# The first modulation in four quarters, and u, k and q in another order, in a hybrid S5, attention and expert block

## The chip, the cores and the metric

One core of one Trainium2 chip runs the whole kernel. It has five engines that run side by side and wait for each other by semaphores: TensorE (PE), VectorE (DVE), ScalarE (ACT), GpSimd (POOL) and SyncE (SP), which here issues nearly all loads. The metric is the device time of one execution in microseconds (us). The time before is 1171.37 us, the median of 3 runs.

## The reference

One block on x (256 tokens x 1024) with a conditioning vector c. The part that matters here is its opening:

```python
cond = jax.nn.silu(c)
mod = cond @ w_ada[l] + b_ada[l]
sh1, sc1, gt1, sh2, sc2, gt2 = jnp.split(mod, 6, axis=-1)
h = modulate(rms_norm(x, g_mix[l]), sh1, sc1)     # h * (1 + sc1) + sh1
proj = h @ w_in[l]                                # [u | q | k | v | gate_A | gate_B], 4096 columns
# u -> S5: complex diagonal state space model, scan over positions
# q, k, v -> 8 heads of causal attention with partial rotary
# then gates, one output projection, and a top-4-of-32 expert FFN
```

All arithmetic is f32. Each weight is read once, some 460 MB in all.

## The kernel before, in words

The program is written engine by engine; the order of the code is the order of execution on each engine, and semaphores link them. Weights come through `ring`, 12 slots of 1 MB: `order` is the order in which SP loads pieces, `use_order` that in which PE uses them up, and SP loads into a slot when its last piece is used.

The first modulation (shift and scale, 2048 columns of w_ada) comes in 8 pieces `("first", 0..7)`, in two halves of four: `first_products(a)` multiplies a piece by `condb` (silu(c), 32 equal columns) in 16 matmuls of 32 x 128 (two records each in the profile). When a half is complete, ACT copies its row out of PSUM (`first_row_copy`), PE turns it into columns (`first_columns`, L550), DVE adds the bias and makes the scale (`first_modulation`, L1448 and L1452), and DVE and ACT make two slices each of `hT`, the modulated x with the model dimension on partitions (L1457 on DVE, `first_hidden` L1155 on ACT). They read x that PE has transposed (`x_columns`, L557).

`proj(g, h)` multiplies one half of the 8 slices k of hT by the weights of group g: 0 is u, 1 q, 2 k, 3 v, 4 to 7 the gates (L609, for v L606). Each slice k of a group is 4 matmuls of 128 x 256 (two records each in the profile). ACT copies a finished group to SBUF (`projected`, L1167). q and k are rotated: PE makes the turned part (`rotate`, L669), DVE combines it with cos and sin (`rotary`, L1494 to L1501).

For the S5 branch, DVE and POOL make tables of cos and sin, `ecos` and `esin`, DVE for the states' first half (LOW) and POOL for the second (HIGH). Level n squares (`square`, L271 to L275) and doubles (`double`, L285 to L290) the table, n = 2, 4, ... 128; at n = 128 the doubling is two rounds of six operations. POOL waits for `phases`, which DVE sets when its own table is finished, before POOL doubles at 128, because of a shared scratch. DVE also makes the discretised B (L1479 to L1481: six operations of 128 x 256, from loaded constants `const_in` and `sprm`); ACT lays it out in blocks (`Bblk`, L1197), PE transposes these (`b_columns`, L650), ACT copies them out. `b_u(j)` (L626) feeds the scan of DVE (`recurrence`).

The small parameters of the S5 branch are turned by PE (L574) and copied by DVE into `sprm` (L1442), which both tables start from.

Behind all this come the gates and the attention, the output projection, and then a loop over the experts, whose weights stream through the same memory.

## Time and profile before

| | |
|---|---|
| median of 3 runs | 1171.37 us (1171.29 to 1172.31) |
| span of the profiled execution | 1171.2 us |
| PE busy | 1126.0 us, 96% |
| DVE busy | 452.4 us, 39% |
| ACT busy | 138.2 us, 12% |
| POOL busy | 107.8 us, 9% |
| moved by DMA | 460.06 MB, mean 393 GB/s |

The profile is that of one execution. The engines overlap, so their busy times do not add up to the span. A timeline row gives the start, the time from the first to the last end of a merged group, the engine, the line and the operation, and in brackets how long the engine was idle before it and what ended this. SPq and ACTq are the issues of DMAs from these engines. Matmuls overlap in the record, so their rate is read from starts, or from a long group: 96 in 20.96 us are 0.218 us each.

### The profile page before, as it was taken

How to read it: one execution, taken by the hardware profiler on the slowest of the kernel's cores; microseconds unless marked ns; L12 is line 12 of the kernel's file. 1: busy time of each engine (PE TensorE's matmuls, PEld its weight loads, DVE VectorE, ACT ScalarE, POOL GpSimd, SP SyncE). 2: the span in 40 equal slices, each digit the busy share in tenths (PEclk: the TensorE clock that was granted, in tenths of full speed). 3: DMA queues.
4: the chain of work that ended last, by engine and by line, in shares of the span. 5: the costliest groups of instructions: out<-in, count | busy, mean ns of one | idle time of the engine just before them, and what ended most of it. 6: DMA issues, size and time to landing. Idle time of an engine off the chain costs nothing.

```text
span 1171.2 us, 17315 instructions
## 1 busy us (share of the span) xinstructions
PE 1126.0 (96%) x7011; PEld 501.6 (43%) x7011; DVE 452.4 (39%) x960; ACT 138.2 (12%) x299; POOL 107.8 (9%) x142
## 2 busy tenths in 40 slices
PE   6999999999999999999999999999999999999996
PEld 5877788554333333333333333333333333333331
DVE  5897767462232222333322232222222222222323
ACT  3213231141000000001000000000000000000002
POOL 2868730000000000000000000000000000000000
PEclk9999999999999999999999999999999999999998
DMA  9993379979999999999999999999999999999994
GB/s 345 317 381 116 108 270 380 418 296 420 428 428 429 430 429 430 431 431 431 435 430 430 430 430 430 431 430 431 431 431 430 430 430 432 433 430 426 426 427 191
DMA packets 49230, 460.06 MB, mean 393 GB/s; under 512 B 8958, under 2 KB 9410, under 8 KB 26924
## 3 DMA queue, kind: packets, MB, share of 16 engines
q1 hardware_dynamic: 48176, 458.19, 93.7%
q10 hardware_dynamic: 1020, 1.38, 0.4%
q8 instruction: 25, 0.41, 0.1%
q14 instruction: 9, 0.07, 0.0%
HBM read 458.51 MB, written 1.05 MB: 392 GB/s over the span
## 4 chain that ended last, share of the span: by engine, by line
PE 74%; DMA 21%; DVE 2%; ACT 1%; issue 1%; SPq 1%; DVEq 0%
PE ps L1038 27%; DMA ring<-in_w_gu 16%; PE ps L1080 16%; PE ps L609 8%; DMA ring<-in_w_down 4%; PE ps L1013 4%; PE ps L957 3%; PE ps L806 2%; PE ps L1060 2%; PE ps L824 2%; PE ps L789 1%; PE ps L881 1%; PE ps L606 1%; DMA ring<-in_w_ada 1%; PE ps L1068 1%
## 5 line engine op out<-in xcount | busy, mean ns | idle before, releaser
L1080 PE MATMUL ps<-ring,tmp 128*64 128x512 f32 x1024 | 227.2, 595 | 11.9 <-ACT tmp L1293 9.7
L1038 PE MATMUL ps<-ring,zone 128*64 128x512 f32 x1024 | 227.2, 596 | 11.1 <-DMA ring<-in_w_gu 11.1
L1038 PE MATMUL ps<-zone 128*64 128x512 f32 x1024 | 227.2, 596 | 0.2 <-DVE zone L1725 0.2
L1792 DVE TENSOR_TENSOR x_tok<-x_tok,ps 128x512 f32<-128x512 f32 x128 | 82.0, 682 | 262.4 <-PE ps L1013 258.9
L1080 PEld LDWEIGHTS ps<-ring,tmp 128*64 128x64 f32 x1024 | 82.8, 137 | 135.6 <-issue 130.8
L1038 PEld LDWEIGHTS ps<-ring,zone 128*64 128x64 f32 x1024 | 70.6, 137 | 163.4 <-issue 142.7
L1038 PEld LDWEIGHTS ps<-zone 128*64 128x64 f32 x1024 | 70.5, 137 | 153.1 <-issue 146.2
L1290 ACT ACTIVATE hT<-hT 128x256 f32<-128x256 f32 x64 | 23.9, 417 | 726.5 <-DVE hT L1807 726.5
L609 PE MATMUL ps<-hT,ring 128*128 128x256 f32 x448 | 101.5, 382 | 0.9 <-DVE hT L1457 0.9
L1807 DVE TENSOR_SCALAR hT<-ps 128x256 f32<-128x256 f32 x64 | 24.2, 420 | 191.7 <-PE ps L1038 191.7
L609 PEld LDWEIGHTS ps<-hT,ring 128*128 128x128 f32 x448 | 83.5, 190 | 14.4 <-issue 4.0
L1786 DVE TENSOR_TENSOR tmp<-ps,zone 128x512 f32<-128x512 f32 x32 | 22.1, 692 | 164.4 <-PE ps L1080 164.4
L1013 PE MATMUL ps<-tmp,xn_tok 64*128 64x512 f32 x248 | 70.0, 641 | 0.0
L957 PEld LDWEIGHTS ps<-ptmp,zone 128*128 128x128 bf16 x1488 | 45.1, 98 | 23.6 <-issue 23.6
L957 PE MATMUL ps<-ptmp,zone 128*128 128x64 bf16 x1488 | 48.8, 194 | 0.0
L1013 PEld LDWEIGHTS ps<-tmp,xn_tok 64*128 64x128 f32 x248 | 18.7, 185 | 50.3 <-issue 50.3
L824 PE MATMUL ps<-cst,ptmp 32*64 32x512 f32 x256 | 34.8, 613 | 0.0
L1000 PE MATMUL ps<-cst,ptmp 32*64 32x512 f32 x128 | 34.4, 613 | 0.0
L1060 PE MATMUL ps<-cst,ptmp 32*64 32x512 f32 x128 | 34.4, 613 | 0.0
L1293 ACT COPY tmp<-ps 128x256 f32<-128x256 f32 x64 | 20.9, 375 | 85.9 <-PE ps L1068 85.9
L806 PE MATMUL ps<-zone,ring 128*128 128x256 f32 x128 | 28.2, 380 | 0.0
L1814 DVE SCALAR_TENSOR_TENSOR hT<-hT 128x256 f32<-128x256 f32 x64 | 27.2, 425 | 2.3
(328 smaller groups left out, 828.7 us busy)
## 6 DMA issues: line engine op xcount, KB each, us to landing
ring<-in_w_down SPq DMA_DIRECT2D x61, 2048.0 KB, 18.7
zone<-in_w_gu SPq DMA_DIRECT2D x23, 4096.0 KB, 28.5
ring<-in_w_gu SPq DMA_DIRECT2D x23, 4096.0 KB, 32.3
zone<-in_w_gu SPq DMA_DIRECT2D x14, 2048.0 KB, 14.0
ring<-in_w_gu SPq DMA_DIRECT2D x13, 2048.0 KB, 15.0
ring<-in_w_ada SPq DMA_DIRECT2D x24, 1024.0 KB, 13.2
ring<-in_w_in SPq DMA_DIRECT2D x16, 1024.0 KB, 14.2
ring<-in_w_gu SPq DMA_DIRECT2D x10, 1024.0 KB, 9.6
```

Of the source, the lines that this page charges most:

```text
L609: last = mm(ps[:, b + m // 2, (m % 2) * T:(m % 2) * T + T], w[:, kk, P * m:P * m + P], hT[:, k, :], start=(k == 0 and m % 2 == 0), stop=(k ...
L806: last = mm(ps[:, b + m // 2, (m % 2) * T:(m % 2) * T + T], w[:, kk, P * m:P * m + P], gluT[:, kk, :], start=(kk == 0 and m % 2 == 0), sto ...
L824: mm(ps[CAP * h:CAP * h + CAP, b, :], hotb[own, :], brow[own, 512 * h:512 * h + 512], start=True, stop=False, skip_group_check=True)
L957: last = mm(ps[:, 2, CAP * f:CAP * f + CAP], xpart[:, c, i, stored(f)], pick[:, i, :], start=(i == 0 and c == 0), stop=(i == TT - 1 and c ...
L1000: last = mm(ps[CAP * h:CAP * h + CAP, 5, :], hotb[3 * EXPERTS:P, :], brow[3 * EXPERTS:P, 0:2 * T], start=True, stop=True, skip_group_check ...
L1013: mm(ps[:, 6 + h, :], pickwT[half, P * t:P * t + P], ysb[half, :], start=True, stop=True).then_inc(S["comb_up"], 1)
L1038: last = mm(ps[CAP * h:CAP * h + CAP, b, :], hg[:, 2 * j + kk, :], w[:, kk, D * b + 512 * h:D * b + 512 * h + 512], start=False, stop=(j = ...
L1060: last = mm(ps[CAP * h:CAP * h + CAP, 3, :], hotb[own, :], brow[own, 512 * h:512 * h + 512], start=True, stop=False, skip_group_check=True)
L1080: last = mm(ps[CAP * h:CAP * h + CAP, 3, :], actT[:, q, j, :], w[:, q, 512 * h:512 * h + 512], start=False, stop=(j == DN_PIECES - 1 and q ...
L1792: V.tensor_tensor(x_tok[:, t, 512 * h:512 * h + 512], x_tok[:, t, 512 * h:512 * h + 512], ps[:, bank + h, :], ALU.add).then_inc(S["comb_ad ...
L1807: V.tensor_scalar(rows_of(gate[:, pair[g]]), down_pair(ps[:, 0, :], g), LIMIT, None, ALU.min).then_inc(S["gated"], 1)
L1814: V.scalar_tensor_tensor(act_[:, pair[g]], up[:, pair[g]], 1.0, gate[:, pair[g]], ALU.add, ALU.mult).then_inc(S["act_set"], 1)
```

## The change

The first modulation is made in four quarters, each of two pieces. A piece now holds four k slices of 256 shift and 256 scale columns, loaded by two DMAs of 0.5 MB with rows of 1 KB instead of one with rows of 2 KB. The x columns are transposed a quarter (two slices) at a time. The weights of u and q come in joint pieces `("uq", 0..3)`, two slices k of both, with rows of 4 KB; `pair_proj` uses them a slice at a time. The first half of k (`proj(2, 0)`) stands ahead of the modulation's last quarter. Then u is finished, then k, then q: ACT copies k before q, and k is rotated first. The banks of PSUM are laid out anew. DVE's square and doubling at 64 and 128 are parted by the modulations of quarters 2 and 3, and the discretised B is made behind the doubling at 128 instead of ahead of it. The bias loads move from ACT's queue to SP's, ahead of the weights; the large constants load two pieces later and in another order. The silu uses exp and a reciprocal on DVE instead of the sigmoid. A row of the S5 parameters is made on POOL. `scores(0)` no longer waits for v, `weigh(0)` does.

```diff
-    order = several("first", 0, 1, 2, 3) + several("in", 0, 2) + several("first", 4, 5, 6, 7) + several("in", 1, *range(3, 15))
+    order = several("first", 0, 1) + several("uq", 0) + several("first", 2, 3) + several("uq", 1) + several("in", 4)
+    order += several("first", 4, 5, 6, 7) + several("uq", 2, 3) + several("in", *range(5, 15))
...
-    use_order = several("first", 0, 1, 2, 3) + several("in", 0) + several("first", 4, 5, 6, 7) + several("in", 2, 1, *range(3, 16))
+    use_order = several("first", 0, 1, 2, 3) + several("uq", 0) + several("first", 4, 5) + several("uq", 1) + several("first", 6, 7)
+    use_order += several("in", 4, 5) + several("uq", 2, 3) + several("in", *range(6, 16))
...
-            half, sc, k4 = n // 4, n % 4 // 2, n % 2
-            return ada[:, 4 * k4:4 * k4 + 4, D * sc + W * half:D * sc + W * half + W]
+            quarter, k4 = n // 2, n % 2
+            both = ada[:, 4 * k4:4 * k4 + 4, 0:2 * D].rearrange("p k (s c) -> p k s c", s=2)
+            return both[:, :, :, T * quarter:T * quarter + T]
+        if kind == "uq":
+            return win[:, 2 * n:2 * n + 2, 0:2 * W]
...
+            sp.dma_start(rows[R_ADA:R_ADA + 2 * KD, :], ada_bias[0:2 * D].rearrange("(k p) -> k p", p=P)).then_inc(more_rows_in, 16)
+            sp.dma_start(rows[R_GMIX:R_GMIX + KD, :], g_mix.rearrange("a (k p) -> (a k) p", p=P)).then_inc(more_rows_in, 16)
+            sp.dma_start(wide_rows[0:8, :], ada_bias[2 * D:6 * D].rearrange("(k p) -> k p", p=RUN * P)).then_inc(more_rows_in, 16)
+            sp.dma_start(wide_rows[8:10, :], g_ffn.rearrange("a (k p) -> (a k) p", p=RUN * P)).then_inc(more_rows_in, 16)
+            sp.dma_start(rows[R_D:R_D + KW, :], ssm_d.rearrange("a (k p) -> (a k) p", p=P)).then_inc(more_rows_in, 16)
...
-                sp.dma_start(slot(n, src.shape[1]), src).then_inc(arrived[n % SLOTS], 16)
+                if kind == "first":
+                    own = slot(n, 4).rearrange("p k (s c) -> p k s c", s=2)
+                    for sc in range(2):
+                        sp.dma_start(own[:, :, sc], src[:, :, sc]).then_inc(arrived[n % SLOTS], 16)
+                else:
+                    sp.dma_start(slot(n, src.shape[1]), src).then_inc(arrived[n % SLOTS], 16)
...
+            for n in range(place["in", 5] + 1):
                 load_piece(n)
-            sp.dma_start(cst[:, P:], const[:, P:]).then_inc(S["const_in"], 16)
             for r, (b, cc) in enumerate(((b_re, c_re), (b_im, c_im))):
                 sp.dma_start(b_in[:, r], b[0].rearrange("(s q) p c -> (q p) s c", q=2)).then_inc(S["const_in"], 16)
                 sp.dma_start(c_in[:, r], cc[0].rearrange("(m g) c p -> (g c) m p", m=KW)).then_inc(S["const_in"], 16)
-            for n in range(place["in", 3] + 1, place["glu", 0]):
+            sp.dma_start(cst[:, P:], const[:, P:]).then_inc(S["const_in"], 16)
+            for n in range(place["in", 5] + 1, place["glu", 0]):
                 load_piece(n)
...
+            def first_columns(quarter):
+
+                pe.wait_ge(S["modrow_sb"], quarter + 1)
+                nc.tensor.transpose(ps[:, 6, mod_cols(quarter)], first_row[quarter], ident).then_inc(S["modT_up"], 1)
+
+            def x_columns(quarter):
+
+                pe.wait_ge(S["xn1"], TT if quarter == 0 else 2 * TT)
+                if quarter == 1:
+                    pe.wait_ge(S["hD_sb"], 1)
+                elif quarter > 1:
+                    pe.wait_ge(S["hD_sb"], quarter)
+                    pe.wait_ge(S["hA_sb"], quarter)
+                    pe.wait_ge(S["mod1_sb"], quarter)
...
+            def pair_proj(g, k, ms=(0, 1, 2, 3)):
+
+                n = take("uq", k // 2)
+                w = slot(n, 2)
+                hidden(k)
+                b = PROJ_BANK[g]
+                if g == 1 and k == 0:
+                    pe.wait_ge(S["sprm_sb"], 1)
+                for m in ms:
+                    last = mm(ps[:, b + m // 2, (m % 2) * T:(m % 2) * T + T], w[:, k % 2, W * g + P * m:W * g + P * m + P], hT[:, k, :],
+                              start=(k == 0 and m % 2 == 0), stop=(k == KD - 1), skip_group_check=True)
+                if g == 0 and k == KD - 1:
+                    last.then_inc(S["u_up"], 1)
+                if g == 1 and k % 2 == 1:
+                    last.then_inc(w_used, 1)
...
-            last.then_inc(more_cols_up, 1)
-            for a in range(1, 3):
-                first_products(a)
-            pe.wait_ge(S["xn1"], TT)
+            last.then_inc(S["cols_up"], 1)
+            first_products(1)
             x_columns(0)
-            first_products(3)
-            pe.wait_ge(S["ssm_rows"], 1)
+            first_columns(0)
+            pe.wait_ge(S["ssm_rows"], 2)
...
-            first_columns(0)
-            x_columns(1)
...
-            proj(0, 0)
+            pair_proj(0, 0)
+            x_columns(1)
+            pair_proj(0, 1)
+            first_products(2)
+            pair_proj(1, 0, (0, 1))
+            first_products(3)
+            pair_proj(1, 0, (2, 3))
+            first_columns(1)
+            pair_proj(1, 1)
+            x_columns(2)
+            pair_proj(0, 2), pair_proj(0, 3)
             first_products(4)
-            for kk in range(3):
-                proj(1, 0, (kk,))
-                first_products(5 + kk)
-            proj(1, 0, (3,), (0, 1))
-            first_columns(1)
-            proj(1, 0, (3,), (2, 3))
-            proj(0, 1)
-            proj(1, 1)
-            proj(2, 0)
+            pair_proj(1, 2)
+            first_products(5)
+            pair_proj(1, 3)
+            first_columns(2)
+            proj(2, 0, (0,))
+            x_columns(3)
+            first_products(6)
+            proj(2, 0, (1,))
+            first_products(7)
+            proj(2, 0, (2,))
+            first_columns(3)
+            proj(2, 0, (3,))
+            for k in range(4, KD):
+                pair_proj(0, k)
+            proj(2, 1)
+            pair_proj(1, 4)
             b_columns()
-            rotate(qT, 0)
+            rotate(kT, 0)
             c_columns(0)
             c_columns(1)
-            proj(2, 1, (0,))
+            pair_proj(1, 5)
             b_u(0)
-            proj(2, 1, (1, 2, 3))
+            pair_proj(1, 6), pair_proj(1, 7)
             proj(3, 0, (0,))
-            rotate(kT, 1)
...
+            act.wait_ge(S["lnD"], 1)
+            link(nc.scalar.activation(stat[:, 1, :], stat[:, 3, :], ACT.Exp))
 
             act.wait_ge(S["cols_sb"], 1)
-            nc.scalar.activation(cond[:, :], cols[:, R_C:R_C + KD], ACT.Sigmoid).then_inc(S["cond_half"], 1)
+            nc.scalar.activation(cond[:, :], cols[:, R_C:R_C + KD], ACT.Exp, scale=-1.0).then_inc(S["cond_half"], 1)
...
                                          scale=cst[:, C_MB + q:C_MB + q + 1]).then_inc(S["Bblk_set"], 1)
-            projected(1, qT)
+            projected(2, kT)
...
                                      scale=(1.0 if r == 0 else -1.0)).then_inc(S[f"CT{r}_sb"], 1)
-            projected(2, kT)
+            projected(1, qT)
             projected(3, v_tok)
...
+            pool.wait_ge(ssm_products, 1)
+            link(nc.gpsimd.tensor_tensor(sprow[:, 13, :], sprow[:, 9, :], are[:, :], ALU.mult))
+            link(nc.gpsimd.tensor_tensor(sprow[:, 14, :], sprow[:, 8, :], aim[:, :], ALU.mult))
+            link(nc.gpsimd.tensor_tensor(sprow[:, 13, :], sprow[:, 13, :], sprow[:, 14, :], ALU.subtract))
+            nc.gpsimd.tensor_tensor(sprow[:, 4, :], sprow[:, 13, :], sprow[:, 10, :], ALU.mult).then_inc(S["ssm_rows"], 1)
...
+                dve.wait_ge(S["mod1_sb"], quarter + 1)
+                k = 2 * quarter
+                V.scalar_tensor_tensor(scale1[:, k:k + 2], mod[:, SC1 + k:SC1 + k + 2], 1.0,
+                                       cols[:, R_GMIX + k:R_GMIX + k + 2], ALU.add, ALU.mult).then_inc(S["scale1_set"], 1)
+                dve.wait_ge(S["scale1_set"], quarter + 1)
+                dve.wait_ge(S["xT_up"], quarter + 1)
+                V.tensor_scalar(hT[:, k, :], xT_bank(k), scale1[:, k:k + 1],
+                                mod[:, SH1 + k:SH1 + k + 1], ALU.mult, ALU.add).then_inc(S["hD_sb"], 1)
...
             dve.wait_ge(S["cols_sb"], 2)
             first_modulation(0)
+            dve.wait_ge(S["sprm_up"], 1)
+            V.tensor_copy(sprm[:, :, :].rearrange("p j s -> p (j s)"), ps[:, 3, 0:5 * ST]).then_inc(S["sprm_sb"], 1)
+            dve.wait_ge(S["sprm_sb"], 1)
             first_phase(V, link, LOW)
             level(2)
-            for n in (4, 8, 16, 32):
+            level(4)
+            first_modulation(1)
+            for n in (8, 16, 32):
                 level(n)
-            first_modulation(1)
-            level(T // 4)
+            square(V, link, T // 4, LOW)
+            first_modulation(2)
+            double(V, link, T // 4, LOW, (tmp[:, 0], tmp[:, 1]))
+            square(V, link, T // 2, LOW)
+            first_modulation(3)
+            double(V, link, T // 2, LOW, (ptmp, probs))
+            V.engine_nop().then_inc(S["phases"], 1)
 
...
-            level(T // 2)
-            V.engine_nop().then_inc(S["phases"], 1)
```

PE from the first weight products on; first the program before. L542 are `first_products`, L557 `x_columns`, L574 the S5 rows, L550 `first_columns`, L609 a projection.

```order
L542 MATMUL ps<-ring,condb 32x128 x16
L562 MATMUL ps<-cst,zone 128x36
L564 MATMUL ps<-cst,zone 128x10 x4
L542 MATMUL ps<-ring,condb 32x128 x32
L557 MATMUL ps<-cst,xn_tok 128x128 x8
L542 MATMUL ps<-ring,condb 32x128 x16
L574 MATMUL ps<-cst,zone 128x16 x5
L550 MATMUL ps<-cst,zone 128x128 x2
L557 MATMUL ps<-cst,xn_tok 128x128 x8
L609 MATMUL ps<-hT,ring 128x256 x16
```

The same place of the changed program, from the second piece on: L567 are `first_products`, L587 `x_columns`, L574 `first_columns`, L622 the S5 rows, L603 `pair_proj`.

```order
L567 MATMUL ps<-ring,condb 32x128 x16
L587 MATMUL ps<-cst,xn_tok 128x128 x4
L574 MATMUL ps<-cst,zone 128x128
L622 MATMUL ps<-cst,zone 128x16 x5
L603 MATMUL ps<-hT,ring 128x256 x4
L587 MATMUL ps<-cst,xn_tok 128x128 x4
L603 MATMUL ps<-hT,ring 128x256 x4
L567 MATMUL ps<-ring,condb 32x128 x16
L603 MATMUL ps<-hT,ring 128x256 x2
L567 MATMUL ps<-ring,condb 32x128 x16
L603 MATMUL ps<-hT,ring 128x256 x2
L574 MATMUL ps<-cst,zone 128x128
```

The first projection stands behind two pieces instead of four, and six pieces and three quarters of the x columns now stand between projections.

DVE from the last half round of the doubling at 128 on, before. L287 to L290 are the doubling, L1484 sets `phases`, L1494 to L1501 are the first rotary (of q).

```order
L287 TENSOR_TENSOR zone<-ptmp,probs 128x4x127
L288 TENSOR_TENSOR ptmp<-zone 128x508
L289 TENSOR_TENSOR probs<-zone 128x508
L290 TENSOR_TENSOR zone<-ptmp,probs 128x4x127
L1484 ISA
L1494 TENSOR_TENSOR tmp<-ps,cst 128x512
L1500 TENSOR_TENSOR zone<-zone,cst 128x512
L1501 TENSOR_TENSOR zone<-zone,tmp 128x512
```

And in the changed program. L294 ends the doubling, L1539 sets `phases`, L1546 to L1548 are the discretised B, L1559 and L1565 the first rotary (of k).

```order
L294 TENSOR_TENSOR zone<-ptmp,probs 128x4x127
L1539 ISA
L1546 TENSOR_TENSOR tmp<-zone,sprm 128x256
L1547 TENSOR_TENSOR tmp<-zone,sprm 128x256
L1548 TENSOR_TENSOR tmp<-tmp 128x256
L1546 TENSOR_TENSOR tmp<-zone,sprm 128x256
L1547 TENSOR_TENSOR tmp<-zone,sprm 128x256
L1548 TENSOR_TENSOR tmp<-tmp 128x256
L1559 TENSOR_TENSOR tmp<-ps,cst 128x512
L1565 TENSOR_TENSOR zone<-zone,cst 128x512
```

The six operations of B have moved from ahead of the square at 128 to between `phases` and the first rotary.

PE around the transposes of B, before: L609 are projections (q's rest, u's second half and k's first), L650 `b_columns`, L669 `rotate` (of q), L660 the transposes of C.

```order
L550 MATMUL ps<-cst,zone 128x128 x2
L609 MATMUL ps<-hT,ring 128x256 x50
L650 MATMUL ps<-cst,zone 128x128 x8
L669 MATMUL ps<-zone,cst 128x256 x4
L660 MATMUL ps<-cst,zone 128x128 x8
L609 MATMUL ps<-hT,ring 128x256 x4
```

And in the changed program: L574 the last `first_columns`, L647 k, L603 u (x16) and q (x4), L688 `b_columns`, L709 `rotate` (of k), L700 the transposes of C.

```order
L574 MATMUL ps<-cst,zone 128x128
L647 MATMUL ps<-hT,ring 128x256 x4
L603 MATMUL ps<-hT,ring 128x256 x16
L647 MATMUL ps<-hT,ring 128x256 x16
L603 MATMUL ps<-hT,ring 128x256 x4
L688 MATMUL ps<-cst,zone 128x128 x8
L709 MATMUL ps<-zone,cst 128x256 x4
L700 MATMUL ps<-cst,zone 128x128 x8
```

What is rotated first is now k, whose projection ends one slice of q ahead of `b_columns`.

## Rows read from the trace of the kernel before

**Rows 1.** The page: PE and DMA busy, in tenths, 40 slices of the span.

```profile
PE   6999999999999999999999999999999999999996
...
DMA  9993379979999999999999999999999999999994
```

**Rows 2.** Timeline of PE, 0 to 45 us: start, us, engine, line, operation.

```profile
9.72 1.93 PE L542 MATMUL ps<-ring,condb 128*32 128x128 f32 x32 [6.29 <-DMA ring<-in_w_ada]
...
15.06 1.93 PE L542 MATMUL ps<-ring,condb 128*32 128x128 f32 x32 [0.71 <-DMA ring<-in_w_ada]
...
21.17 0.44 PE L550 MATMUL ps<-cst,zone 128*128 128x128 f32 x2
21.45 1.04 PE L557 MATMUL ps<-cst,xn_tok 128*128 128x128 f32 x8
22.83 7.15 PE L609 MATMUL ps<-hT,ring 128*128 128x256 f32 x32 [0.35 <-DVE hT L1457]
29.91 1.08 PE L542 MATMUL ps<-ring,condb 128*32 128x128 f32 x32
```

**Rows 3.** Windows: stretch, length, busy time of each engine, PEclk, DMA share, GB/s.

```profile
4.00:6.60 2.60, 0.00 (x0) 0.00 (x0) 0.46 (x2) 2.22 (x3) 0.00 (x0) 1.00 1.02 403
7.00:14.00 7.00, 4.28 (x69) 3.62 (x69) 5.00 (x17) 6.22 (x12) 0.00 (x0) 1.00 1.06 387
```

**Rows 4.** Timeline of PE, 42 to 170 us.

```profile
42.53 20.96 PE L609 MATMUL ps<-hT,ring 128*128 128x256 f32 x96 [0.59 <-DVE hT L1457]
63.32 1.04 PE L650 MATMUL ps<-cst,zone 128*128 128x128 f32 x8
64.19 1.89 PE L669 MATMUL ps<-zone,cst 128*128 128x256 f32 x8
```

**Rows 5.** Timeline of DVE, 0 to 130 us.

```profile
28.66 0.18 DVE L271 TENSOR_TENSOR zone<-zone 128x8 f32<-128x8 f32 x1
...
38.83 0.42 DVE L290 TENSOR_TENSOR zone<-tmp 128x248 f32<-128x248 f32 x1
...
42.75 0.45 DVE L271 TENSOR_TENSOR zone<-zone 128x8 f32<-128x8 f32 x1
...
44.47 0.68 DVE L285 TENSOR_TENSOR tmp<-zone 128x504 f32<-128x504 f32 x1
...
47.34 1.41 DVE L289 TENSOR_TENSOR tmp<-zone 128x504 f32<-128x504 f32 x1
...
51.62 1.15 DVE L1480 TENSOR_TENSOR tmp<-zone,sprm 128x256 f32<-128x256 f32 x1
...
55.40 0.43 DVE L1480 TENSOR_TENSOR tmp<-zone,sprm 128x256 f32<-128x256 f32 x1
...
66.19 0.69 DVE L1494 TENSOR_TENSOR tmp<-ps,cst 128x512 f32<-128x512 f32 x1
```

**Rows 6.** Timelines of ACT and SP: the first and last of five small loads; ring and constants.

```profile
2.12 0.44 ACTq L1119 DMA_DIRECT2D zone<-in_b_ada  x1
...
3.91 0.41 ACTq L1123 DMA_DIRECT2D zone<-in_ssm_d  x1
...
2.06 3.83 SPq L390 DMA_DIRECT2D ring<-in_w_ada  x4
...
42.74 2.43 SPq L426 DMA_DIRECT2D zone<-in_ssm_c_im  x1
```

**Rows 7.** Timeline of POOL, 0 to 95 us.

```profile
21.42 0.11 POOL L296 MEMSET zone<- 128x8 f32 x1 [20.50 <-DVE sprm L1442]
...
46.73 1.48 POOL L285 TENSOR_TENSOR zone<-zone 128x504 f32<-128x504 f32 x1
...
66.25 1.04 POOL L285 TENSOR_TENSOR zone<-zone 128x508 f32<-128x508 f32 x1 [9.31 <-DVEq L1484]
```

**Rows 8.** Timeline of ACT, 42 to 130 us.

```profile
56.31 0.91 ACT L1197 ACTIVATE zone<-tmp,cst 128x256 f32<-128x256 f32 x2 [1.42 <-DVE tmp L1481]
57.13 0.99 ACT L1167 COPY zone<-ps 128x1024 f32<-128x1024 f32 x1
```

181 lines of the change are left out of this document (82 added, 99 removed).

## The prediction

> **What bounds the kernel now.** I read the page first, for where time can be lost at all. TensorE (PE) is busy throughout all but the first and the last of 40 slices, and the DMA engines are full from the opening to about 90 us and again from about 150 us on; between the two they idle because the ring of weights is full [rows 1]. So up to there PE sets the pace, the transfers are released by PE's use of the ring, and a delay of PE in the first 100 us should move everything behind it by the same amount, the expert loop included, whose first transfers also wait for PE to free their slots. Then the timelines of the opening, engine by engine. PE begins its weight products at 9.72, waits for a transfer once more before 15.06, and starts the first projection at 22.83; in the stretch that is changed it then waits only once, 0.59 us for DVE at 42.53 [rows 4]. Its early work is slow: 32 products took 1.93 us at 15.06 and 1.08 at 29.91 [rows 2], which is TensorE at 1.2 and at 2.4 GHz (the clock column of the windows prints 1.00 all the same [rows 3]); the rise comes about 21.3, as the transposes from 21.45 on run at the fast rate (8 in 1.04) and the two before them at the slow one, after PE has worked without a break since 15.06. Last DVE's timeline against PE's: DVE ends its phase tables just before 66.19, where it takes up the rotary of q, whose rotation PE made from 64.19 [rows 4, 5]. DVE has no reserve at this point, and this is the place the forecast turns on.
>
> **Start of the first projection.** Five small loads now stand ahead of the weights on SP; on ACT the same five took from 2.12 to 4.32, 2.2 us [rows 6]. The weights were issued from 2.06, the x load before them filled the engines until about 6.6 (1.05 MB at 403 GB/s [rows 3]), and from issue to flow there are some 2 us, so an issue at 4.3 to 4.8 leaves a bubble of about 0.2 us. The first modulation's weights now come in rows of 1 KB. Rows of 4 KB (x) ran at 403 GB/s and rows of 2 KB at 387 [rows 3]: with 16 engines that is 162.6 and 84.7 ns a row, so 45.7 ns for 1 KB by a straight line, 358 GB/s, 2.93 us a piece instead of 2.67 (two pieces between 9.72 and 15.06 [rows 2]). Bounds: 2.67, and 5.4 if a short row cost what a 2 KB row does. I take 2.93, as the two rates differ little. The Trainium skill (DMA: Bandwidth & Descriptors, Specifications) says that 512 B are enough for line rate; by it the start comes 0.5 us earlier. The two measured rates already differ above that size, so I keep the line.
>
> Piece 0 is then there at 10.2 and piece 1, which completes the first quarter, at 13.1. PE: products 1.93 (15.05), 4 transposes of x 0.98 (twice their share of the 1.04), one transpose 0.22, then 1.2 us through mod, scale and the first hT as between the transposes' end at 21.61 and 22.83 [rows 2]: 17.6 with the semaphores, 5.2 us earlier than before. The table load of the sigmoid and the bias loads leave ACT and cost nothing, as PE waits for transfers meanwhile.
>
> **PE from there.** What now lies behind 17.6 is more: up to the transposes of B there are 21 slices of projection (u 8, k 8, q 5) at 1.74 (96 matmuls in 20.96 [rows 4], 8 a slice) = 36.5; six firsts at 1.03 = 6.2; three pairs of x columns at 0.5 and three row transposes at 0.23 = 2.2. Together 44.9, so 62.5. Before, the same point was at 63.32 [rows 4] with one q slice less, so 65.06 for the same work. The gain is 2.6 us, not 5.2. The slow clock takes part of it: if it rises at about 21.3 as before, 3.7 us at half speed lose 1.85. Bounds 0 (rises at once) and 3.1 (6.2 us after 17.6, as after 15.06). Left: a gain of 0.75 before waits.
>
> **DVE.** The row transpose of quarter 1 ends 8.0 + 1.85 after 17.6, at 27.45; DVE is free by then. Modulation 1.0; levels 8 to 32 took 28.66 to 39.25, 10.6 [rows 5]; square of 64 took 42.75 to 44.44, 1.7. POOL is released by sprm, now 3.6 us earlier (17.85 for 21.42 [rows 7]), so DVE meets wider POOL operations; +0.4. Quarter 2's modulation (0.9) ends at 42.05. PE reaches the x columns of quarter 3 at 27.45 + 13.2 = 40.65 and waits there: **1.4 us**. Behind that wait stand the last two firsts, and everything.
>
> The doubling of 64 shows what POOL does to DVE: the same shape took 0.68 at 44.47 and 1.41 at 47.34, once POOL had begun its own at 46.73 [rows 5, 7]. Before, 2 of 6 were slow (5.75 in all). POOL's now begins about 43, DVE's 42.05: 4 of 6 slow, 7.2, to 49.25. Square of 128 with POOL still at it: 1.1 + 0.8 = 1.9. Modulation of quarter 3: 1.0, to 52.15; PE needs its hT only at 53, no wait. Doubling of 128: 12 times 0.68 + 0.04 = 8.65 (as at 44.47 [rows 5]), to 60.8. At that instant DVE lets POOL into its own doubling of 128 (the 9.31 us that POOL waited [rows 7]), and DVE's next work is now the six B operations. Beside POOL these took 1.15 (51.62), alone 0.43 (55.40) [rows 5]; before, four of six were slow, now all: 6 times 1.19 = 7.1, to 67.9. Bounds 2.7 and 8.7 (0.43 each, and 1.41 as the slow 504-wide ones). ACT's second pair of B blocks 0.95, then the copy of k 1.0 [rows 8]: both stand in that order on ACT, so k is ready at **69.9**.
>
> **PE again.** It reaches the transposes of B at 62.5 + 1.85 + 1.4 = 65.75, can do the first half, and the rotation of k would start at 66.6. It starts at 69.9: **3.3 us**. Before, the rotation began at 64.19, 65.95 with the q slice. Sum: **+3.95 us** (-2.6 + 1.85 + 1.4 + 3.3). Behind it the order repeats that of before with one q slice less before the second rotation; DVE, spared POOL's company there since POOL ends earlier, keeps up. The last of the constants' loads was issued until 45.2 [rows 6]; two pieces (5.3) and the shorter rows (2.1) later that is 52.6, and with as long to land as the first weights (2.06 to 9.72) they are in by 60.3, just before DVE's 60.8: nothing, and up to 1 us if I am late by that. The moved q and k only exchange banks and places: nothing. Own time: the profiled execution's span was 1171.2, so 1175.15; the median of the runs shown, 1171.37, lies 0.2 above that span, so 1175.3.
>
> A rule that weighs on this term: the Trainium skill (SBUF — State Buffer, its rules on the shared port pair) says that a DVE instruction with two SBUF inputs and a GpSimd one that reads SBUF exclude each other, the second blocked until the first finishes. That the pair excludes agrees with 1.15 against 0.43. Full blocking at each step would make the second rival below's slow end; the row at 51.62 is shorter than a whole POOL operation and its own run.
>
> **Rivals.**
> 1. *DVE keeps its old durations* (no more company of POOL than before). The B operations take 6.1, the doubling of 64 5.75, the square 1.1: k is ready 3.25 us earlier, at 66.65, and the rotation, due at 66.6, hardly waits. The gain of the opening is eaten by the clock and the wait at quarter 3: +0.7, 1172.1. For it: POOL may drift out of step. Against: POOL's start of the 128 doubling hangs on the very step behind which B stands.
> 2. *Longer waits.* Each B operation sits out a whole POOL operation (1.04 at 66.25, 1.48 at 46.73, so 1.26 [rows 7]) and then runs 0.43: 10.1 instead of 7.1, +3.0. Or PE's pause of 3.3 us drops its clock to the lower level for as long as in the opening, +3.1. Either gives 1178.3. Against the first: the row at 51.62; against the second: the pauses of before were shorter, so nothing shows it.
> 3. *Faster.* PE's clock is up at 17.6 and DVE is nowhere waited for: -2.6, 1168.8. For it: the start is really earlier. Against: DVE had no time left at 66.19, and it now has two more modulations, stands idle before 27.45 for want of quarter 1, and has ACT's two steps behind its last work.
>
> **Chances.** Forecast 0.48 (own range 1173.6 to 1177.2), rival 1 0.28, rival 2 0.11, rival 3 0.09, something else 0.04. About 0.2% (2.3 us) is what a measurement of this kernel tells from no change. Faster takes rival 3 and a part of the rest, 0.12; same rival 1 and the near edge of the forecast, 0.32; slower 0.56. The range takes in rivals 1 and nearly 2: 1169.6 to 1178.2.
>
> **What would show it.** First projection at about 17.6 (later than 19: the 1 KB rows or the issues). Eight matmuls of a slice near 3.5 us until about 21, then 1.74. PE idle for DVE's or ACT's hT at the x columns of quarter 3, some 1.4 us. B operations near 1.15 each behind the doubling of 128, PE idle some 3 us between the B transposes and the rotation of k, released by ACT. Wrong if the B operations run at 0.43, if PE stands less than 1 us before that rotation, or if the gap found there is closed again before 250 us.

## The result, and the profile after

| | before | changed |
|---|---|---|
| median | 1171.45 us (4 runs, 1171.29 to 1172.31) | 1181.89 us (4 runs, 1178.93 to 1185.07) |
| span of the profiled execution | 1171.2 us | 1182.4 us |
| PE busy | 1126.0 us | 1130.9 us |
| moved by DMA | 460.06 MB, mean 393 GB/s | 460.06 MB, mean 389 GB/s |

The changed kernel is slower: ratio 1.009, 95% interval 1.0075 to 1.0104. That is +10.4 us where +3.95 was forecast. The time of a run lies 1.8 to 1.9 us above its span in every run that lists both, and the spans of the changed kernel run from 1177.1 to 1183.2, a spread of 6 us where the times of before spread over 1. Its four runs form two pairs, 1178.93 and 1179.59, 1184.19 and 1185.07. The profiled one is 1184.19, of the slower pair, so what follows reads one of the longer two; its 11.2 us only happen to lie near the 10.4 of the medians.

To place the loss, one row serves as a mark behind the whole changed part: the 32 matmuls of the second expert's second product. Timeline of PE, before and then changed; what stands behind it is alike, so a delay here is nearly all of the delay.

```profile
306.47 7.09 PE L1080 MATMUL ps<-ring,tmp 128*64 128x512 f32 x32 [0.33 <-ACT tmp L1293]
```

```profile
317.39 7.09 PE L1138 MATMUL ps<-ring,tmp 128*64 128x512 f32 x32 [0.33 <-ACT tmp L1350]
```

10.9 us of the 11.2 by which the spans differ are lost before this row. Timeline of PE, changed kernel, the rows that answer to [rows 2]. L567 are `first_products`, L587 `x_columns`, L574 `first_columns`, L603 u and q, L647 k.

```profile
13.32 1.94 PE L567 MATMUL ps<-ring,condb 128*32 128x128 f32 x32
...
17.71 3.69 PE L603 MATMUL ps<-hT,ring 128*128 128x256 f32 x8 [0.55 <-DVE hT L1514]
21.23 0.60 PE L587 MATMUL ps<-cst,xn_tok 128*128 128x128 f32 x4
21.67 1.89 PE L603 MATMUL ps<-hT,ring 128*128 128x256 f32 x8
...
27.54 0.27 PE L574 MATMUL ps<-cst,zone 128*128 128x128 f32 x1
```

The first projection starts at 17.71, runs at half speed (3.69 for the eight matmuls of a slice) until 21.2 and then at the full rate (1.89). Up to here all is as forecast. Then the rows that answer to [rows 4]: L688 are the transposes of B, L709 the rotation of k, L664 `b_u`.

```profile
39.25 1.89 PE L647 MATMUL ps<-hT,ring 128*128 128x256 f32 x8
46.14 1.08 PE L587 MATMUL ps<-cst,xn_tok 128*128 128x128 f32 x4 [4.99 <-ACT hT L1208]
47.15 1.94 PE L567 MATMUL ps<-ring,condb 128*32 128x128 f32 x32
49.02 3.41 PE L647 MATMUL ps<-hT,ring 128*128 128x256 f32 x8
52.36 1.08 PE L567 MATMUL ps<-ring,condb 128*32 128x128 f32 x32
...
72.58 1.04 PE L688 MATMUL ps<-cst,zone 128*128 128x128 f32 x8
73.55 1.99 PE L709 MATMUL ps<-zone,cst 128*128 128x256 f32 x8
...
101.25 1.13 PE L664 MATMUL ps<-zone 32*128 32x256 f32 x8 [1.67 <-DVE zone L1598]
...
103.57 8.59 PE L647 MATMUL ps<-hT,ring 128*128 128x256 f32 x32
```

PE reaches the x columns of quarter 3 at 41.1 and stands for 5.0 us. The products behind the pause take 1.94 us where the full rate gives 1.08, the slice at 49.02 takes 3.41 where it gives 1.89. From 52 on nothing is waited for until the third `b_u` at 101.25: 1.7 us, and again slow matmuls (8.59 for 32 where [rows 2] has 7.15). Ahead of k's rotation at 73.55 there is no wait. The same in windows, columns as in [rows 3]; the clock is the third number from the end.

```profile
36.00:40.00 4.00, 4.00 (x47) 3.17 (x46) 3.72 (x9) 0.27 (x1) 3.53 (x7) 1.00 1.07 371
44.00:48.00 4.00, 1.86 (x20) 1.50 (x24) 3.86 (x6) 0.56 (x1) 3.77 (x4) 0.64 0.94 248
48.00:52.00 4.00, 4.00 (x31) 3.04 (x20) 3.86 (x5) 0.00 (x0) 3.69 (x5) 0.51 0.54 73
101.00:105.00 4.00, 3.75 (x24) 2.77 (x25) 1.34 (x4) 0.92 (x1) 3.50 (x3) 0.77 0.60 242
105.00:109.00 4.00, 4.00 (x17) 3.42 (x16) 3.93 (x7) 1.72 (x8) 3.77 (x4) 0.81 0.00 0
```

Behind each of the two pauses it falls to the lower of TensorE's two levels. What that costs is read against the same work at the full rate in another kernel. Timeline of PE in e8, then in e6 (both described below):

```profile
39.32 0.60 PE L587 MATMUL ps<-cst,xn_tok 128*128 128x128 f32 x4
...
42.78 1.08 PE L567 MATMUL ps<-ring,condb 128*32 128x128 f32 x32
```

```profile
93.65 1.13 PE L664 MATMUL ps<-zone 32*128 32x256 f32 x8
...
102.86 1.07 PE L678 MATMUL ps<-zone 128*32 128x256 f32 x16
```

From the x columns to the second product behind them the changed kernel takes 6.2 us (46.14 to 52.36) against 3.5 in e8, so 2.75; from the third `b_u` to the y columns (L678, the first product behind POOL's part of the scan) 10.85 (101.25 to 112.09) against 9.2 in e6, so 1.65. The sum from before: start and early clock -0.75 as forecast, 5.0 + 2.75 at quarter 3, 1.65 + 1.65 at the third `b_u`: +10.3 at the mark, where 10.9 were found.

Who is late? Timeline of ACT, the row of its hT for quarter 2, which PE is said to wait for.

```profile
45.32 0.56 ACT L1208 ACTIVATE hT<-ps,mod,scale 128x256 f32<-128x256 f32 x1 [7.61 <-DVE scale L1510]
```

ACT waited 7.6 us for DVE's scale. So DVE, timeline of the changed kernel, in answer to [rows 5]:

```profile
28.78 0.17 DVE L275 TENSOR_TENSOR zone<-zone 128x8 f32<-128x8 f32 x1
...
41.57 0.17 DVE L275 TENSOR_TENSOR zone<-zone 128x8 f32<-128x8 f32 x1
41.78 0.97 DVE L276 TENSOR_TENSOR zone<-zone 128x8 f32<-128x8 f32 x1
42.78 0.18 DVE L277 TENSOR_TENSOR zone<-zone 128x8 f32<-128x8 f32 x1
42.99 0.90 DVE L278 TENSOR_TENSOR zone<-zone 128x8 f32<-128x8 f32 x1
43.93 0.18 DVE L279 TENSOR_TENSOR zone<-zone 128x8 f32<-128x8 f32 x1
44.15 0.16 DVE L1506 TENSOR_TENSOR mod<-ps,cols 128x4 f32<-128x4 f32 x1
44.34 0.90 DVE L1510 SCALAR_TENSOR_TENSOR scale<-mod,cols 128x2 f32<-128x2 f32 x1
45.27 0.54 DVE L1514 TENSOR_SCALAR hT<-ps,scale,mod 128x256 f32<-128x256 f32 x1
45.73 1.15 DVE L289 TENSOR_TENSOR tmp<-zone 128x504 f32<-128x504 f32 x1
...
65.10 0.42 DVE L1546 TENSOR_TENSOR tmp<-zone,sprm 128x256 f32<-128x256 f32 x1
65.56 1.15 DVE L1547 TENSOR_TENSOR tmp<-zone,sprm 128x256 f32<-128x256 f32 x1
...
70.50 1.15 DVE L1548 TENSOR_TENSOR tmp<-tmp 128x256 f32<-128x256 f32 x1
```

The square of 64 (41.57 to 44.11) is five operations of eight elements a partition. Three take 0.18 us, two take 0.97 and 0.90, and the scale at 44.34, two elements from SBUF, again 0.90. The operations ahead of it and behind it, which read PSUM, take their usual 0.16 and 0.54. Timeline of POOL at that time:

```profile
41.68 1.04 POOL L289 TENSOR_TENSOR zone<-zone 128x504 f32<-128x504 f32 x1
42.80 1.07 POOL L290 TENSOR_TENSOR zone<-zone 128x504 f32<-128x504 f32 x1
43.95 1.27 POOL L291 TENSOR_TENSOR zone<-zone 128x504 f32<-128x504 f32 x1
```

POOL had just begun its 504-wide operations, 1.04 to 1.27 us each. The three slow DVE operations each begin inside one of them and end within 0.03 us of its end. How the two engines fall into step differs between executions: in e4 and e7 below, which are alike up to here, the square's operations took 0.17 to 0.22, the 248-wide ones ahead of them took 0.71 to 0.88 where they take 0.42 alone, and PE waited 2.8 us instead of 5.0.

### The profile page after: what moved, and what is told of

Read it like the earlier page. It is cut to its first block, busy times and chain, and to the rows that moved or that the text cites. A ratio compares the mean times of both kernels' runs of the same rounds, so it can differ in the third digit from the quotient of the medians.

```text
span 1182.4 us, 17362 instructions
## 1 busy us (share of the span) xinstructions
PE 1130.9 (96%) x7011; PEld 504.5 (43%) x7011; DVE 459.2 (39%) x964; ACT 137.7 (12%) x301; POOL 109.3 (9%) x146
## 2 busy tenths in 40 slices
DMA packets 52430, 460.06 MB, mean 389 GB/s; under 512 B 9086, under 2 KB 17730, under 8 KB 30124
## 3 DMA queue, kind: packets, MB, share of 16 engines
HBM read 458.51 MB, written 1.05 MB: 389 GB/s over the span
## 4 chain that ended last, share of the span: by engine, by line
PE 71%; DMA 21%; DVE 5%; issue 1%; ACT 1%; SPq 1%; DVEq 0%; ACTq 0%
PE ps L1096 27%; DMA ring<-in_w_gu 16%; PE ps L1138 16%; PE ps L647 6%; DMA ring<-in_w_down 4%; PE ps L1071 4%; PE ps L1015 3%; PE ps L864 2%; PE ps L1118 2%; PE ps L882 2%; PE ps L603 1%; PE ps L847 1%; PE ps L939 1%; PE ps L1126 1%; ACT tmp L1350 1%
## 5 line engine op out<-in xcount | busy, mean ns | idle before, releaser
L647 PE MATMUL ps<-hT,ring 128*128 128x256 f32 x320 | 75.5, 393 | 0.0
L647 PEld LDWEIGHTS ps<-hT,ring 128*128 128x128 f32 x320 | 61.8, 197 | 10.2 <-issue 2.0
L603 PE MATMUL ps<-hT,ring 128*128 128x256 f32 x128 | 31.9, 400 | 0.6 <-DVE hT L1514 0.6
```

The costliest lines, as they stand in the source:

```text
L603: last = mm(ps[:, b + m // 2, (m % 2) * T:(m % 2) * T + T], w[:, k % 2, W * g + P * m:W * g + P * m + P], hT[:, k, :], start=(k == 0 and m ...
L647: last = mm(ps[:, b + m // 2, (m % 2) * T:(m % 2) * T + T], w[:, kk, P * m:P * m + P], hT[:, k, :], start=(k == 0 and m % 2 == 0), stop=(k ...
```

## The experiments

The forecast had allowed 0.4 us for this company at quarter 3, and 1.4 us of wait. The theory: DVE and POOL share one budget of time, that is, each operation of one can hold up the other; every wait of the changed kernel is a piece of it, and the clock takes its part behind each pause. The rivals: DVE's order alone (A), a new cost of the order itself (B). All diffs are against the changed kernel unless said otherwise. The mark is the row shown above; waits are PE's idle times from 20 us to the mark, over 0.5 us, in order of time. Waits, clock and mark are those of the one profiled execution.

| run | median us (runs) | ratio to before, 95% | waits of PE | clock falls | mark |
|---|---|---|---|---|---|
| changed | 1181.89 (4) | 1.0075 to 1.0104 | 4.99, 1.67 | twice | 317.39 |
| e1 | 1182.63 (4) | 1.008 to 1.0114 | 2.59, 1.52 | twice | 315.58 |
| e2 | 1179.90 (4) | 1.0052 to 1.0086 | 0.98, 3.92 | once | 313.31 |
| e3 | 1180.57 (4) | 1.0051 to 1.0085 | 0.68, 1.68 (fill 4.4) | once | 317.05 |
| e4 | 1176.79 (4) | 1.0031 to 1.0064 | 2.77, 2.06 | no | 311.28 |
| e5 | 1179.45 (4) | 1.0056 to 1.0087 | 0.67, 1.19, 3.04, 0.56 | once | 313.26 |
| e7 | 1176.54 (5) | 1.0033 to 1.0071 | 2.76 | no | 307.14 |
| e6 | 1173.77 (11) | 1.0009 to 1.0027 | 0.66, 0.57 | no | 308.08 |
| e8 | 1179.95 (5) | 1.0054 to 1.0081 | 3.80 | once | 312.51 |
| e9 | 1180.44 (4) | 1.0067 to 1.0108 | 2.30, 2.02, 1.62, 1.05 | twice | 314.45 |
| e10 | 1178.50 (5) | 1.0047 to 1.0075 | 0.53, 3.83, 1.12 | once | 313.21 |
| e12 | 1178.47 (5) | 1.0038 to 1.0066 | 2.72, 0.63 | once | 312.62 |
| e13 | 1177.26 (5) | 1.0030 to 1.0057 | 0.51, 2.69, 0.85 | once | 311.25 |
| e14 | 1172.52 (11) | 1.0001 to 1.0019 | 1.49 | no | 308.02 |
| e15 | 1171.52 (12) | 0.9993 to 1.0011 | 1.47, 0.92 | no | 306.53 |
| e16 | 1172.46 (11) | 0.9995 to 1.0013 | 0.84 | no | 306.84 |
| e17 | 1171.68 (11) | 0.9990 to 1.0008 | 0.53, 0.84, 0.93 | no | 306.01 |
| e11, on before | 1171.41 (11) | 0.9990 to 1.0008 | 0.57 | no | 305.87 |

**e1, quarter 2's modulation earlier in DVE's order.**

```diff
-            for n in (8, 16, 32):
+            for n in (8, 16):
                 level(n)
-            square(V, link, T // 4, LOW)
+            square(V, link, 32, LOW)
             first_modulation(2)
+            double(V, link, 32, LOW, (tmp[:, 0], tmp[:, 1]))
+            square(V, link, T // 4, LOW)
```

> The modulation of quarter 2 stands on DVE between square and doubling of level 32 instead of behind the square of 64. Theory A (DVE reaches that modulation too late; the wait and the clock drop behind it are the first 8 us): PE's wait of 5.0 us at the x columns of quarter 3 falls under 1 us, the slow matmuls behind it (about 3 us lost) go, and PE reaches the transposes of B some 7 us earlier, at 65 to 66. DVE is no faster, so it now has PE wait for k: 3 to 5 us before the rotation of k, and the wait for the scan before the third b_u stays near 1.7. Time 1175 to 1179, 3 to 8 below the changed kernel. Rival B (the cost lies behind the opening, in DVE's total work, and a wait only moves): the time stays within 2 us of the changed kernel, 1180 to 1184.

The wait at the x columns is gone, and 2.59 us at quarter 3's hT and 1.52 at B stand in its place, each with a slow stretch behind it. The time did not fall, as rival B had it. DVE is late as a whole, not in its order.

**e2, POOL held back.** POOL waits for quarter 2's modulation, and its two casts of the mask move ahead of its doubling of 128.

```diff
             for n in (2, 4, 8, 16, 32):
+                if n == 8:
+                    pool.wait_ge(S["hD_sb"], 3)
                 square(nc.gpsimd, link, n, HIGH)
```

> POOL starts its level 8 only when DVE has made hT of quarter 2, and makes the two mask copies before its doubling of 128; nothing else differs. Theory A1 (DVE is late at quarter 2 because its operations with two inputs in SBUF wait for POOL's): levels 8 to 32 take 9.3 us instead of 12.8, the square of 64 1.1 instead of 2.5, and PE's wait at the x columns of quarter 3 falls from 5.0 to under 1; time 1172 to 1177. Rival A2 (DVE is late by its own work, two more modulations and the idle time before quarter 1): levels 8 to 32 keep at least 12 us, the wait stays above 3.5 us and the time above 1179.

With POOL out of the way PE waits nowhere until 90.85 and is at the transposes of B at 63.07. For the same work, with one slice more, the kernel before would be there at 65.06; of the 2 us between them 1.8 are owed to a clock that rose earlier in this execution. So POOL's company is the cause of DVE's lateness. The time, 1179.90, is not the 1172 to 1177 expected, for the price comes later: timeline of PE in e2.

```profile
63.07 1.04 PE L688 MATMUL ps<-cst,zone 128*128 128x128 f32 x8
...
104.05 1.93 PE L678 MATMUL ps<-zone 128*32 128x256 f32 x16 [3.92 <-POOL zone L1424]
...
107.92 5.98 PE L647 MATMUL ps<-hT,ring 128*128 128x256 f32 x16
```

POOL's products of the scan are now 3.9 us late, and the sixteen matmuls at 107.92 take 5.98 for 3.72.

**e3, the pause filled.** 18 matmuls that add zeros stand where PE waits for quarter 2.

```diff
             proj(2, 0, (0,))
+            for _ in range(18):
+                mm(ps[:, 0, 0:144], ident, hot[:, :, :].rearrange("p a b -> p (a b)"), start=False, stop=False, skip_group_check=True)
             x_columns(3)
```

> PE makes 18 more matmuls of 128 x 144 (36 records of some 0.12 us, 4.4 us in all) that add zero to a bank, just before the x columns of quarter 3, where it waits 5.0 us. Theory C (the pause itself drops the clock, and what follows runs at 1.2 GHz for some 6 us): the records after the wait are at full rate, 8 of a slice in 1.74 instead of 3.4, PE is at the transposes of B some 3 us earlier (about 69.5), and the time is 2 to 4 us under the changed kernel's. Rival (the slow records come from something else, such as DVE or POOL activity or the load): they stay, and the time is the same or longer.

PE works through the 4.4 us, and what follows runs at the full rate: the clock fell because of the pause. PE was at the transposes of B at 69.44, 3.1 us earlier than the changed kernel (72.58). The clock stayed up until the next real pause, 1.68 us at the third `b_u`, behind which 32 matmuls took 9.06. So most of the gain went again: from there to the y columns 12.48 us for 9.2, and the mark came only 0.3 us earlier. The median fell by 1.3 us, less than the 2 to 4 expected, and the two intervals overlap.

**e4, POOL's first product of the scan behind the second rotary.**

```diff
+                if j == 0:
+                    pool.wait_ge(S["rope_set"], 2)
                 pool.wait_ge(S["scanned"], 4 * j + 4)
```

> POOL's first product of the scan (six operations of 128 x 512) waits until the second rotary is done. Theory D (DVE's second rotary meets it, 7.0 us instead of 5.2, and so the second scan ends 1.7 us late for PE's third b_u, with a clock drop behind it): second rotary 5.3 us, the wait of 1.7 us before the third b_u goes, no slow matmuls around 101 to 108; time 1.5 to 3.5 us below the changed kernel. Rival (the second scan is late because the second rotation now comes 1.7 us of PE work earlier than before and DVE's chain is as long as it is): the wait stays above 1 us, time within 1 us of the changed kernel.

The third `b_u` is not waited for, as expected, and the time falls by 5.1 us, more than the 3.3 us of that wait and the slow matmuls behind it. The rest lies at quarter 3: 2.77 us here against 4.99, and no fall of the clock behind it, though nothing was changed ahead of it. How DVE's and POOL's operations interleave there differs between executions, which goes with the spread of the changed kernel's runs; that it makes all of the spread is not shown.

**e5, a shorter hold of POOL.**

```diff
                 square(nc.gpsimd, link, n, HIGH)
+                if n == 32:
+                    pool.wait_ge(S["hD_sb"], 3)
                 double(nc.gpsimd, link, n, HIGH, (xs[:, 0, 0], xs[:, 0, 1]))
```

> Edit: POOL waits, between its square and its doubling of level 32, until the modulation of quarter 2 is made; nothing else is changed. Theory A (DVE is late at quarter 3 because each of its small operations waits for a wide one of POOL): DVE's square of 64 takes about 1.1 us instead of 2.5 and the levels before it about 1 us less, PE waits under 1 us at the x columns of quarter 3 and keeps its clock there. A pause of 2 to 3 us at the columns of B or at the rotation of k takes its place, and the wait of 1.7 us at the third b_u stays, since DVE's B operations and second rotation still have POOL beside them: 1175 to 1178 us. Rival (the wait is made by DVE's own work or by ACT's row copy): the wait stays at 3 to 5 us, 1180 to 1183.

The square of 64 takes 1.05 us and PE waits 0.67. But POOL's held-back work now meets DVE's doubling of 64 and of 128, and B is late twice: 1.19 and 3.04. I had expected 2 to 3 in all and 1175 to 1178; the wait moved and grew.

**e7, POOL let in behind B instead of ahead of it** (with e4's edit).

```diff
             double(V, link, T // 2, LOW, (ptmp, probs))
-            V.engine_nop().then_inc(S["phases"], 1)
...
                 dve.wait_ge(S["Bsum_set"], r + 1)
+            V.engine_nop().then_inc(S["phases"], 1)
```

> Edit: DVE lets POOL into its doubling of 128 behind the six operations of B instead of ahead of them; and POOL's first product of the scan waits for the second rotation, as in the run e4. Theory (the term of the forecast that charged POOL's company at B): the six operations take about 2.6 us (0.43 each) instead of 6.5, ACT's blocks are there before PE wants them, the wait of 2.1 us at the columns of B is gone, and the time is about 2 us under that of e4: 1174 to 1175.5. Rival (POOL's table, let in some 3 us later, is late itself): PE waits for POOL's half at the fifth b_u, some 3 us, and the time is that of e4 or above: 1176.5 to 1180.

This prices POOL's company at B, for which the forecast charged 7.1 us instead of 2.7. Timeline of DVE in e7, B's first and last operation:

```profile
61.09 0.42 DVE L1547 TENSOR_TENSOR tmp<-zone,sprm 128x256 f32<-128x256 f32 x1
...
63.39 0.43 DVE L1549 TENSOR_TENSOR tmp<-tmp 128x256 f32<-128x256 f32 x1
```

2.7 us for the six, where the changed kernel took 6.55 (65.10 to 71.65). e4's wait of 2.06 at B is gone. The median, 1176.54, is that of e4 all the same and not the 1174 to 1175.5 expected, with runs from 1172.94 to 1180.42; the profiled one is the fastest of them and shows no late POOL, as the rival had it. The mechanism is shown in the trace, the gain in the median is not.

**e6, the three together** (e5's, e7's and e4's edits).

> Edit: the three together: POOL waits inside level 32 for quarter 2's modulation, is let into the doubling of 128 behind B, and makes its first scan product behind the second rotation. If the added time of the changed kernel is all made by POOL's company on DVE and by the pauses and clock that follow from it, PE waits nowhere before 110 us by more than 1 us, and the time is that of before less the 0.75 us by which the start is earlier, and up to 2.6 us less than before: 1169 to 1172. Rival (something else in the new order costs time, for example q beside v, or the scan): no wait in the opening and still 1174 or more.

1.5 us of waits are left, and +2.3 us: no wait over 1 us, as expected, and still above the 1169 to 1172. The mark can be reckoned: 306.47 - 0.75 + 0.66 + 0.57 + 0.24 (a short one before k's rotation) = 307.2, against 308.08. Most of the ten microseconds were waits and the clock behind them. Of the 0.9 left over 0.2 lie in the opening (the k slice ahead of quarter 3's x columns starts at 39.35 here, at 39.14 in e16), and some 0.2 at each pause, as the idle time is counted from the end of a row that overlaps the next one in a stretch without pause.

**The kernel before, again.**

> The kernel before, unchanged, profiled a second time. The changed kernels' times lie 1.8 us above the spans of their profiles, the first profile of before was 0.2 us below its median. If that profile was of an execution some 1.6 us longer than its fellows, the span is now near 1169.6; if the offset is a property of the kernel, near 1171.2.

The span is 1169.2. So the first profile was of an execution longer than its fellows. In part this is the opening: PE's clock was up before 18.74 here, where in the first profile it rose only during the products at 18.82, and the mark lies at 305.58 for 306.47. The rest lies at the very end, the last eight wide matmuls of PE, first profile and then second:

```profile
1160.14 3.46 PE L1110 MATMUL ps<-tmp,xn_tok 64*128 64x512 f32 x8 [2.00 <-issue]
```

```profile
1159.20 1.99 PE L1110 MATMUL ps<-tmp,xn_tok 64*128 64x512 f32 x8 [1.79 <-issue]
```

Behind a pause near 2 us the clock had fallen in the one and not in the other. The same row took 3.56 in the changed kernel. The changed kernels show the same two cases in the opening; e6 had the late one, e2 and e5 the early one, which is worth 1.8 us to them.

**e8, POOL held one square later than in e2.** Expected to mend e2's end.

```diff
             for n in (2, 4, 8, 16, 32):
                 square(nc.gpsimd, link, n, HIGH)
+                if n == 8:
+                    pool.wait_ge(S["hD_sb"], 3)
```

> Edit: as e2 (POOL's table late, casts of the mask ahead of its doubling of 128), but POOL waits for quarter 2's modulation one square later, between its square and its doubling of level 8. In e2 these five small squares took 3.4 us behind the pause. Theory (DVE and POOL share one budget of time; what one is spared the other pays): PE waits nowhere before the third b_u by over 1 us, the third b_u waits about 1 us for DVE, and the 3.9 us for POOL's products at the y columns shrink to about 0.5, without the drop of the clock behind them: 1172 to 1174.5, some 6 us under e2. Rival (the pause of e2 was not what made POOL late there): the wait at the y columns stays over 3 us, 1178 to 1180.

A miss. POOL still ended 3.8 us late, and the sixteen matmuls behind the pause took 6.39 for 3.72. It ended 1.2 us earlier than in e2 (102.77 for 103.99): of the 3.4 us saved at the hold the rest was lost beside DVE's doublings of 64 and 128. And PE, not held at the third `b_u` any more, came 1.1 us earlier.

**e9 to e11, the opening filled.** PE has nothing to do until the first weights land at 10.4.

```diff
+            for _ in range(20):
+                mm(ps[:, 7, 0:P], ident, ident, start=True, stop=True, skip_group_check=True)
             pe.wait_ge(S["cond_set"], 1)
...
             last.then_inc(S["cols_up"], 1)
+            for _ in range(5):
+                mm(ps[:, 7, 0:P], ident, ident, start=True, stop=True, skip_group_check=True)
             first_products(1)
```

> Edit: the changed kernel with PE filled in the opening, where it waits for the first weights: 20 matmuls of the identity by itself (128x128) behind the first transpose, 5 more ahead of the second piece's products, into a bank of PSUM that nothing reads before it is written anew. Theory (the first slices are slow because PE's clock rises only behind unbroken work): products and transposes before 17.7 run at the fast rate, the first projection starts at about 16.4 and runs at 1.74 to 1.97 a slice, so PE is ahead by 1.3 us (where the clock had risen early anyway) to 3.2. DVE's work starts with PE's columns, so its wait stays as it is: 1178.5 to 1181. Rival (the early slow rate is not from the clock's idle time, or the transfers bind): no change, 1181 to 1183.

> Edit: e8 and e9 together. If both theories hold, the gains add up, as long as the transfers keep up: 1.3 to 3.2 us under e8, 1169.5 to 1172. Rival (transfers or the constants of B then bind): DVE's first B operation waits for the constants, or PE for a piece of weights, and the time is that of e8.

> Edit: the kernel before with the same fill of the opening. Its first projection comes at 22.8 behind a piece that lands at about 18 (2.67 us behind the third), so only products, transposes and what lies behind that piece can be faster: 0.9 us where the clock rose late (before against its second profile), near 0.4 else, and 1170.5 to 1171.5. Rival: the fill delays the first piece's products, or drains nothing, 1171.5 to 1172.5.

Timeline of PE in e9:

```profile
10.36 1.08 PE L569 MATMUL ps<-ring,condb 128*32 128x128 f32 x32 [0.87 <-DMA ring<-in_w_ada]
...
16.68 1.96 PE L605 MATMUL ps<-hT,ring 128*128 128x256 f32 x8 [1.03 <-DVE hT L1518]
```

The first projection starts at 16.68 instead of 17.71 and at the full rate. The medians fall by 1.45 us (changed to e9, e8 to e10), near the low end of what was expected; the intervals of e9 and the changed kernel overlap. e10 keeps e8's late POOL (3.83) and so stays far above the 1169.5 to 1172 expected. On the kernel before it does nothing: its fourth piece comes at 18.9 whatever the clock.

The fill has a price of its own. In all five filled versions of the changed kernel (e9, e10, e13, e15, e17), and in no other profile, ACT's issue of one load took 1.23 to 1.50 us instead of 0.44, and PE then stood 0.85 to 1.12 us ahead of L820, late in the table's waits. Timelines of ACT in e14 and e15, which is e14 filled, and of PE in e15:

```profile
172.95 0.44 ACTq L1279 DMA_DIRECT2D cst<-in_b_down  x1
```

```profile
170.60 1.30 ACTq L1283 DMA_DIRECT2D cst<-in_b_down  x1
```

```profile
183.56 1.06 PE L820 MATMUL ps<-zone,ones 128*32 128x512 f32 x8 [0.92 <-issue]
```

ACT's next operations come later by that much, then DVE's, and L820 reads what DVE adds up. Why the issue is longer is not shown; it takes back up to 1 us of what the fill gives.

**e12 and e13, DVE and POOL kept apart.** POOL is held behind the square of 16, then again until B is made; the mask is cast by ACT. e13 adds the filled opening.

```diff
             square(nc.gpsimd, link, T // 4, HIGH)
+            pool.wait_ge(S["phases"], 1)
             double(nc.gpsimd, link, T // 4, HIGH, (xs[:, 0, 0], xs[:, 0, 1]))
             square(nc.gpsimd, link, T // 2, HIGH)
-            pool.wait_ge(S["phases"], 1)
```

> Edit: the changed kernel with the work of DVE and POOL kept apart: POOL waits for quarter 2's modulation between its square and its doubling of level 16, then, ahead of its doubling of 64, until DVE has made its whole table and B; the two casts of the mask go to ACT. In e8 POOL's last product of the scan's second quarter ended 3.8 us after PE wanted it, and the clock drop behind this cost some 4.5 us more. Here POOL has level 8 and the square of 16 behind it at the pause and no casts, about 3 us, so PE waits there 0 to 1 us and keeps its clock, and nowhere else over 1 us: 1171.5 to 1173.5, and the measured +10 us of the change are then all waits and clock. Rival (the waits only move again: B or the third b_u late instead): 1175 to 1180.

> Edit: e12 with PE filled in the opening as in e9. The fill took 1.45 us off both e8 and the changed kernel. If the waits are gone the two add up, 1170 to 1172, at or just under the kernel before. Rival: PE, ahead by more, meets DVE or POOL again and the gain is eaten, 1172 to 1175.

A miss again. POOL stood idle for 5.8 us ahead of that doubling, and then ended 2.7 us too late. I had counted its work ahead of the second hold, but from its release at 61.74 to its end at 103.6 POOL works without a break, so the moment of its release sets its end. e13, 1177.26, is outside both of its expectations.

**e14 to e17, the release earlier.** POOL is let in behind the first half of B, held only ahead of its doubling of 32, and DVE makes quarter 2's modulation ahead of the square of 64. e16 moves POOL's square of 128 into its idle time; e15 and e17 are e14 and e16 with the opening filled.

```diff
             square(nc.gpsimd, link, T // 4, HIGH)
+            pool.wait_ge(S["Bsum_set"], 1)
             double(nc.gpsimd, link, T // 4, HIGH, (xs[:, 0, 0], xs[:, 0, 1]))
...
-            square(V, link, T // 4, LOW)
             first_modulation(2)
+            square(V, link, T // 4, LOW)
```

> Edit: as e12, but POOL waits for quarter 2's modulation only ahead of its doubling of 32, is let into its doubling of 64 behind the first half of B instead of behind all of it, and DVE makes quarter 2's modulation ahead of the square of 64. In e12 POOL stood idle for 5.8 us before that doubling and ended 2.7 us too late for PE. Here DVE's doubling of 128 has no company (1.1 us) and the release comes 1.3 us earlier again, so POOL ends 2.4 us earlier: the wait at the y columns is 0.3 us or less, PE's clock stays up, nothing else over 0.7 us. e12 less 2.7 of wait and 3.1 of slow clock: 1172 to 1173.5, that is the balance of the new order without its waits, +1 us at most on before. Rival (the order costs by itself, or the waits move once more): 1175 to 1178.5.

> Edit: e14 with PE filled in the opening as in e9. Without waits the fill's gain (1.2 to 1.9 us so far) should stand in full: 1170.5 to 1172, level with the kernel before. Rival: PE meets a late engine, 1172 to 1176.

> Edit: as e14, but POOL makes its square of 128 in the 11.2 us in which it stands idle ahead of the doubling of 64 (the square needs only the entry that the square of 64 made). In e14 the square took 1.8 us behind that pause, and PE waited 1.5 us for POOL at the y columns. Theory (what is left over is this wait): the wait is gone, 1171.0, level with the kernel before or up to 0.7 us under it. Rival (a further engine is late next): 1172 to 1173.

> Edit: e16 with PE filled in the opening. e15's wait of 1.5 us at the y columns is gone too: 1169.7 to 1170.5, under the kernel before by 0.1%. Rival: 1171 to 1172, as e15.

e14 comes to 1172.52, 0.1% above before, and e15 to 1171.52, both as expected, though POOL is still 1.5 us late. Rows of e14 and then of e16, timeline of PE:

```profile
102.82 1.07 PE L678 MATMUL ps<-zone 128*32 128x256 f32 x16 [1.49 <-POOL zone L1424]
```

```profile
92.19 1.13 PE L664 MATMUL ps<-zone 32*128 32x256 f32 x8 [0.84 <-DVE zone L1600]
...
101.40 1.07 PE L678 MATMUL ps<-zone 128*32 128x256 f32 x16
```

In e16 POOL's wait is gone, DVE is late by 0.84 at the third `b_u`, and the clock is up throughout. Its mark by the reckoning is 306.47 - 0.75 + 0.84 = 306.6; measured 306.84. The account closes. e14's gives 307.2 for 308.02, and the 0.8 left over are in the opening: it was at the x columns of quarter 3 at 41.64, e16 at 40.87, as its first weights came 0.2 us later and its clock rose later. For e17, whose clock is up from the start, the whole -2.6 counts: 306.47 - 2.6 + 0.53 + 0.84 + 0.93 = 306.2; measured 306.01.

But the medians of e16 and e17 did not fall under those of e14 and e15; both lie in the range of their rivals. In e17 a new wait of 0.53 us for weights and the 0.93 at L820 are part of it. Behind the mark single losses come and go: e14, e15 and e17 lose 1.0 to 1.5 us at one expert between 555 and 587 us to a wait for weights, e16 0.1. e17's profiled execution is the slowest of its eleven; its span is 1.7 us longer than e15's, by a wait of 1.13 us for weights at 1136 and the last eight matmuls at the lower rate (3.61 for 1.99). What makes an execution meet these losses is not shown. No version beats the kernel before; e15 to e17 are level with it.

## Why the prediction was wrong

**Right.** The start: 17.6 forecast, 17.71 measured. The row transpose of quarter 1 at 27.45: 27.54. That 5.2 us of earlier start are worth some 0.75: in e16, without its wait of 0.84, PE is at the y columns at 100.56, and before at 101.15, so 0.6. The six B operations: 7.1 forecast, 6.55 measured. That ACT's second blocks and the copy of k stand one behind the other: 71.69 and 72.50.

**Right by luck.** The clock rose at 21.2, near the 21.3 of the forecast, which was a misreading of before. The two transposes that I took to be at half rate take 0.44 in the second profile of before too, where the clock is already up; in the first, the products at 18.82 took 1.85 for 1.93, so it rose near their end, at about 20.5. In other executions with the same opening it was up at the first projection (e5, at 17.66).

**The step that failed** is "Quarter 2's modulation (0.9) ends at 42.05 ... waits there: 1.4 us". It ended at about 45.8, and the term of 1.4 measured 5.0, with the clock behind it 7.75. Three sizes in it were off. Levels 8 to 32 took 12.8 us (28.78 to 41.54) for 11.0, the square of 64 2.54 for 1.7, the modulation 1.7 for 0.9. I had priced wide operations beside wide ones, from 0.68 against 1.41 [rows 5], and taken narrow ones as nearly free. They are not: 0.18 us became 0.97. The forecast's own rows had a sign of it, 0.45 us for eight elements at 42.75 in [rows 5]. The Trainium skill (SBUF — State Buffer, SBUF: two separate sides) has a DVE instruction with two SBUF inputs and a GpSimd one that reads SBUF block each other fully: the one that starts first keeps the other out. The rows at 41.78 and 42.99 agree, as they end with POOL's operations; I had cited that rule for B only and set it aside there. e2 shows the cause: without POOL the same point is reached without a wait. Where DVE's narrow operations were spared (e4, e7) the wait was still 2.8, twice the forecast.

**The clock.** Rival 2 held that a pause of 3.3 us might drop the clock, at +3.1, and got little weight because no pause of before was long enough to show it. It dropped, at another place, behind 5.0 us: 2.75. e3 shows that the pause is the cause.

**"DVE, spared POOL's company there since POOL ends earlier, keeps up."** Wrong: POOL ended its doubling at 81 and took up its first product of the scan at 88.05, beside DVE's second rotary. Timelines of POOL and DVE, changed kernel:

```profile
88.05 1.27 POOL L1417 TENSOR_TENSOR zone<-zone 128x512 f32<-128x512 f32 x1 [6.00 <-DVE zone L1598]
```

```profile
89.90 1.64 DVE L1566 TENSOR_TENSOR zone<-zone,tmp 128x512 f32<-128x512 f32 x1
```

The rotary's six operations took 7.0 us. Before, they took 5.24, in e4 without company 4.3. The third `b_u` was 1.67 late, with 1.65 of slow matmuls behind it. e4 removes both.

**The wait before k's rotation.** 3.3 us were forecast and none was seen. Not because DVE was earlier (its last B operation ended at 71.65, for 67.9 forecast, after it had itself waited 2.4 us for PE ahead of quarter 3's modulation), but because PE was later still: k's copy ended at 73.49, and the rotation began at 73.55. Where PE is earlier it appears, at the transposes of B just ahead of it: 1.52 in e1, 2.06 in e4, 3.04 in e5. So the place was read rightly, but the overlap was not: a pause of PE ahead of it takes the place of this one, and the two do not add up.

**The reference point.** I took the span 1171.2 as lying 0.2 us under the median; the profiled execution was a long one, and time less span is 1.8 to 1.9 us. As only the difference of +3.95 was at stake, this moved the forecast by nothing.

**What e6 and e14 to e17 add.** With most of its waits gone the new order is level with the old one, not ahead. The earlier start is mostly paid back by the slow clock of the opening, or by the fill's own price where that is avoided, and DVE and POOL together have no time to spare. That is the time of rival 1, reached by keeping POOL away, not by a POOL out of step; for the kernel as it stands it was wrong. One correction to the text ahead of the prediction: by the code POOL's wait for `phases` guards no shared scratch, DVE's doubling of 128 uses `ptmp` and `probs`, POOL's `xs`; it only sets the order. The experiments moved it to later points only.

## What to carry to other kernels

Where two engines work side by side on SBUF, price their shared stretch as one budget, narrow operations too, and look at what each repair of one does to the other's last deadline. Find the engine whose finish is waited for next and how much it is late; removing a wait of PE on an engine without reserve moves the wait. A pause of PE may cost as much again in the slow matmuls behind it (2.75 us behind 4.99, 4.5 behind 3.80, 3.3 behind 1.68) or nothing at all (behind 2.77 in e4), so a wait forecast at a few microseconds is to be charged with that as a range.

## What the runs showed of the hardware

Pauses of PE and the clock behind them: after 0.98, 1.47 and 1.49 us it stayed up (e2, e15, e14). After 3.04, 3.80, 3.83, 3.92 and 4.99 it fell to the lower level. Between, the length alone did not decide: it fell after 1.52, 1.62, 1.67, 1.68, 2.02, 2.59, 2.69 and 2.72, and stayed up after 2.06, 2.30, 2.76 and 2.77. Ahead of the last eight matmuls PE stood 1.5 to 2.2 us in every kernel; they took 3.35 to 3.61 us in six profiles (clock 0.51 in 1161 to 1164 us of before) and 1.99 in the other fourteen. Each fall cost 1.4 us (behind 2.02 in e9) to 4.5 (behind 3.80 in e8). The Trainium skill (TensorE: Matmul & The Clock Gate, HAM oscillation) describes a kernel whose clock falls anew at every wait for the next weights. The traces agree that the fall can come more than once, twice in the changed kernel, but here it did not come at every wait.

In the opening the clock rose at different moments with the same work ahead of it: in the two profiles of the kernel before the same products took 1.85 and 1.08 us, and in the changed kernels the first eight matmuls took 3.5 to 3.75 us in some, 1.97 in others. With PE filled from 3.3 us on they took 1.96 to 1.99 each time.

Where rows of 1 KB were loaded, the rate was 348 to 355 GB/s (windows 15 to 20 and 30 to 35 us of the changed kernel and six others), against 385 and 386 in the same windows of before, 387 for rows of 2 KB and 403 for 4 KB [rows 3]. 358 had been drawn by a straight line.
